# A state-space part stepped four tokens at a time, with prepared power matrices and a local term

## The reference, cut to what matters

```
lam_bar = jnp.exp(lam * dt)
b_bar = ((lam_bar - 1.0) / lam)[:, :, None] * b_mat
bu = jnp.einsum('gph,blgh->blgp', b_bar, u)
# states[t] = lam_bar * states[t-1] + bu[t]
y = jnp.einsum('ghp,blgp->blgh', c_mat, states).real
y = y + d_skip * u
y = jax.nn.gelu(y)
y = y * jax.nn.sigmoid(y @ w_glu + b_glu)
```

## Time and profile before

| | |
|---|---|
| median of three runs | 2754.56 us |
| lowest, highest | 2746.49, 2756.39 us |
| span of the profiled execution | 2747.2 us |
| its own time | only the span is given, inside the range of the runs |
| TensorE (PE) busy | 2600.3 us, 95% |
| VectorE (DVE) busy | 2165.5 us, 79% |
| ScalarE (ACT) busy | 1483.6 us, 54% |
| GpSimd (POOL) busy | 947.8 us, 34% |
| bytes moved by DMA | 670.58 MB, 243 GB/s from HBM over the span |

### The profile page before, as it was taken

One profiled execution on the slowest core, in us unless ns is written; L12 is line 12 of the kernel. 1 busy time (PEld: TensorE's weight loads), 2 busy tenths in 40 slices (PEclk: granted clock), 3 DMA queues, 4 the chain that ended last, 5 costly groups with the idle time before them and its releaser, 6 DMA issues. The chain is left out here.

```text
span 2747.2 us, 47482 instructions
## 1 busy us (share of the span) xinstructions
PE 2600.3 (95%) x17802; PEld 2379.0 (87%) x17802; DVE 2165.5 (79%) x2488; ACT 1483.6 (54%) x1930; POOL 947.8 (34%) x586
## 2 busy tenths in 40 slices
PE   8999899999998998888998978999999999999997
PEld 7999699999897998658998747999999999999986
DVE  5667666766787676987855997898989898989888
ACT  4337543443434334424334515777777777777765
POOL 6990089688789992126900130000000000000000
PEclk9999999999999998999999988999999999999999
DMA  8664267566566653324553415999999999999985
GB/s 309 252 237 148 103 241 256 202 250 254 191 241 229 220 183 134 115 105 164 183 184 138 164 63 192 343 350 333 352 335 349 338 347 343 347 345 346 340 320 216
DMA packets 129209, 670.58 MB, mean 244 GB/s; under 512 B 14672, under 2 KB 14992, under 8 KB 80064
## 3 DMA queue, kind: packets, MB, share of 16 engines
q1 hardware_dynamic: 111024, 604.72, 59.9%
q0 software_dynamic: 18064, 64.21, 6.9%
HBM read 667.82 MB, written 1.05 MB: 243 GB/s over the span
## 5 line engine op out<-in xcount | busy, mean ns | idle before, releaser
L1721 PE MATMUL work<-xT_hi,wh_gu 128*128 128x256 f32 x2088 | 593.9, 284 | 21.6 <-DVE xT_lo L985 12.0
L1722 PE MATMUL work<-xT_lo,wh_gu 128*128 128x256 f32 x2088 | 592.3, 284 | 0.0
L1723 PE MATMUL work<-xT_hi,wl_gu 128*128 128x256 f32 x2088 | 591.7, 283 | 0.0
L1721 PE MATMUL work<-wh_gu,mixT_hi 128*128 128x256 f32 x1792 | 507.5, 283 | 2.8 <-DVE wl_gu L1439 1.5
L1722 PE MATMUL work<-wl_gu,mixT_hi 128*128 128x256 f32 x1792 | 505.8, 282 | 0.0
L1723 PE MATMUL work<-wh_gu,mixT_lo 128*128 128x256 f32 x1792 | 505.5, 282 | 0.0
L857 DVE TENSOR_TENSOR wl_gu<-raw_gu,wh_gu 128x2048 fp32r<-128x2048 f32 x158 | 392.3, 2483 | 72.0 <-ACT wh_gu L395 71.5
L1721 PEld LDWEIGHTS work<-xT_hi,wh_gu 128*128 128x128 f32 x2088 | 401.3, 192 | 30.1 <-issue 21.3
L1722 PEld LDWEIGHTS work<-xT_lo,wh_gu 128*128 128x128 f32 x2088 | 401.7, 192 | 4.8
L1723 PEld LDWEIGHTS work<-xT_hi,wl_gu 128*128 128x128 f32 x2088 | 401.5, 192 | 0.0
L862 DVE TENSOR_TENSOR wl_d<-raw_d,wh_d 128x1024 fp32r<-128x1024 f32 x157 | 250.2, 1594 | 189.6 <-ACT wh_d L402 189.5
(11 more groups left out here) (436 smaller groups left out, 4785.6 us busy)
## 6 DMA issues: line engine op xcount, KB each, us to landing
raw_gu<-in_w_gu SPq DMA_DIRECT2D x271, 1024.0 KB, 5.2
raw_d<-in_w_d SPq DMA_DIRECT2D x269, 512.0 KB, 5.4
scratch<-in_w_gu SPq DMA_DIRECT2D x112, 1024.0 KB, 7.2
scratch<-in_w_d SPq DMA_DIRECT2D x112, 512.0 KB, 7.8
scratch<-in_w_mod POOLq DMA_DIRECT2D x96, 512.0 KB, 3.7
scratch<-in_s_b POOLq DMA_DIRECT2D x16, 256.0 KB, 2.9
rows<-in_norm_post POOLq DMA_DIRECT2D x6, 512.0 KB, 4.4
rows<-in_ln_g POOLq DMA_DIRECT2D x4, 512.0 KB, 5.5
```

Of the source, the lines that this page charges most:

```text
L1721: pe.matmul(out_, w[0], m[0], start=start, stop=False)
L1722: pe.matmul(out_, w[0], m[1], start=False, stop=False)
L1723: return pe.matmul(out_, w[1], m[0], start=False, stop=stop)
```

## The change

It takes the recurrence four tokens at a time (STEP = 4). With 64 blocks of four tokens c, the state behind each block is scanned with lam_bar^4, and

- the input of a block is one product of the four tokens' u (`U4`: 4 x 32 channels on 128 partitions, 64 columns) by B times lam_bar^(3-j) (`BF`),
- the output of a block is lam_bar^(i+1) times the factor and C (`CW`, 4 x 32 outputs) by the state behind the block before, plus a local term of the four tokens by each other, with D on its diagonal (`LOCAL`, 128 x 128 a tile), by `U4`.

`BF`, `LOCAL` and `CW` are prepared in the dense block before each mixer. For that the last 12 steps of the first of these dense blocks and the last 22 of the second are written out in place of the loop (`tail`); r counts back from the end of the first, and in the second everything comes ten steps earlier. Behind the gate/up product of step r, ahead of the down product:

- r = -11: TensorE transposes B (8 transposes), ScalarE keeps it (2 evictions of 512), and POOL multiplies it by lam_bar three times (18 operations of 512 elements).
- r = -7 to -4: TensorE waits for these powers, and transposes them, 8 a step (32), ScalarE keeps them, 2 evictions a step.
- r = -3: TensorE multiplies the powers by the scaled C: one 512-wide matmul for D, 32 of 32 columns. ScalarE keeps the result in steps -3 and -2, seven pieces each, and POOL makes `CW`, 24 operations of 512.

POOL loads B with eight and C with one DMA a layer and scales C (`s5_matrices`); the seven operations for it on VectorE go, and the DMAs for each round too. The table of angles has 64 columns in place of 256. It is built inside the mixer, after x is ready, beside the attention part (six doublings, seven squarings). Conversion of U+6 moves on VectorE from level 6 to behind the state-space part. The rest of the part is two halves h of eight state tiles:

- ScalarE `spread(h)`: 16 copies of 32 partitions by 2 x 64 out of PSUM into `U4`, after the table is there and after u0 and u1 (h = 0), u2 and u3 (h = 1). Blocks u2 and u3 lie in the banks of the output gate now, and wait for its Silu.
- TensorE `bu(h)`: 16 matmuls of 64 columns. VectorE `turn_in(h)`: four products of 8 x 64; `scan(h)`: two sums and 16 scans of 64; `turn_back(h)`: three operations; POOL the same three for the other component.
- TensorE `outputs(h)`: 8 matmuls of 64 and 16 of 63 columns.
- ScalarE `gathered_back(h)`: 16 Gelu pieces out of PSUM into `YT`, then the high part; VectorE its low part.

Buffers in scratch are laid out anew. The core of the diff:

```diff
+STEP = 4
+TAIL, LEAD = 12, 10
             def ffn(n0, dyn, nf, f0, fdyn):
+                tail = TAIL + LEAD * PREPARED.index(n0) if n0 in PREPARED else 0
...
+                for r in range(nf - tail, nf):
+                    gate_up(n0 + r)
+                    s5_products(PREPARED.index(n0), r - nf + LEAD * PREPARED.index(n0))
+                    down(n0 + r - 1, 0, f0 + r - 1, 0, False, False)
+                if tail:
+                    pe.wait_ge(s["local_sb"], 14 * (PREPARED.index(n0) + 1))
...
+            def s5_products(n, r):
+                if r == -11:
+                    pe.wait_ge(s5b_in, 128 * (n + 1))
+                    for c in range(2):
+                        for t in range(4):
+                            last = pe.transpose(PB[:, 2 + c, t * P:(t + 1) * P], BRAW[:, t, c, :], ident)
+                        last.then_inc(s["bt"], 1)
+                if -7 <= r <= -4:
+                    for k in (2 * r + 14, 2 * r + 15):
+                        c, st = turned_input(k)
+                        pe.wait_ge(s["powers"], n + 1)
+                        if k >= 2:
+                            pe.wait_ge(s["bf_sb"], 8 * n + k - 1)
+                        for i in range(4):
+                            last = pe.transpose(PB[:, 2 + k % 2, i * P:(i + 1) * P], stack(c, st.start + i), ident)
+                        last.then_inc(s["bf"], 1)
+                if r == -3:
+                    pe.wait_ge(s["bf_sb"], 8 * n + 7)
+                    pe.wait_ge(s["c_ready"], n + 1)
+                    pe.matmul(PB[:, 2, :], ONTO, SKIP, start=True, stop=False)
+                    for st in range(16):
+                        for c in range(2):
+                            last = pe.matmul(PB[:, 2, 32 * st:32 * st + 32], stack(c, st), CP[:, c, st, :],
+                                             start=False, stop=st == 15 and c == 1)
+                    last.then_inc(s["local"], 1)
...
+                def spread(h, used, count):
+                    act.wait_ge(s["table"], n + 1)
+                    act.wait_ge(used, count)
+                    ps = PA[:, 2 * h:2 * h + 2, 0:S].rearrange("p t (c j) -> p t j c", j=STEP)
+                    to = U4.rearrange("p (t q) c -> p t q c", q=4)
+                    for q in range(4):
+                        for j in range(STEP):
+                            act.activation(to[32 * j:32 * j + 32, 2 * h:2 * h + 2, q, :], ps[32 * q:32 * q + 32, :, j, :],
+                                           ACT.Copy).then_inc(s["u4"], 1)
...
+                dve.wait_ge(s["table"], n + 1)
                 turn_in(0)
-                for r in range(8):
...
+                scan(0)
+                dve.wait_ge(g["o"], n + 1)
+                turn_in(1)
+                gated_heads()
+                turn_back(0)
+                scan(1)
+                turn_back(1)
+                mixed_heads()
+                lo(U + 6)
+                lo(U + 7)
+                result_lo(0)
+                result_lo(1)
                 lo(U + 8)
...
                 bu(0)
                 heads()
                 bu(1)
                 heads_transposed()
                 r_ = [row_of(k) for k in (6, 7, 4, 5, 3, 0, 1, 2)]
-                for r in range(8):
...
+                outputs(0)
+                outputs(1)
+                pe.wait_ge(gu_lo, U + 7)
+                pe.wait_ge(s["bu_used"], 2 * (n + 1))
+                pe.wait_ge(mix_l, MSTART[b] + 2)
+                r_[0](U + 6, 0).then_inc(gu_used, 1)
                 pe.wait_ge(d_lo, U + 7)
                 r_[1](U + 6, 2).then_inc(d_used, 1)
-                pe.wait_ge(s["yl"], n + 1)
-                pe.wait_ge(s["ysum"], 4 * (n + 1))
+                pe.wait_ge(s["yl"], 2 * (n + 1))
```

More of the change, by code:

```diff
@@ L193, in program @@
         GO = first_net.rearrange("p (t d) -> p t d", t=NT)
[L194 to L204, removed]
+        OG = GO
+        PP = [[x.rearrange("p (t c) -> p t c", t=8) for x in half] for half in (
+            [view(1536 + 512 * i, 512) for i in range(5)] + [BT],
+            [ROW[:, 512 * i:512 * i + 512] for i in range(6)])]
+        YT = view(512, 1024).rearrange("p (k s) -> p k s", k=4)
         GL = view(2048, 1024).rearrange("p (k s) -> p k s", k=4)
@@ L517, in ffn, with step @@
             def ffn(n0, dyn, nf):
[L519 to L524, removed]
-                if n0 == 0:
-                    steps(0)
-                with act.Fori(1 if n0 == 0 else 0, nf // 2) as j:
-                    steps(dyn + j * 2)
+                def step(n, at):
+                    hi_gu(n + 1, at)
+                    ge(act, gu_used, n + 1, at)
+                    act.activation(SG[n % 2], PB[:, n % 2, 0:S], ACT.Silu).then_inc(silu_done, 1)
+                    hi_d(n + 1, at)
@@ L1079, in ffn @@
                     first, steps, reg = 1, chain.n, chain.reg
-                with dve.Fori(0, nf // 2 - first) as j:
+                tail = TAIL + LEAD * PREPARED.index(n0) if n0 in PREPARED else 0
+                looped = (nf - tail) // 2 - first
+                with dve.Fori(0, looped) as j:
                     chain.n, chain.reg = steps, reg + j * 4
@@ L1083, in ffn @@
                         step(r, j * 2)
-                chain.n, chain.reg = steps + 4 * (nf // 2 - first), reg
+                chain.n, chain.reg = steps + 4 * looped, reg
+                for r in range(nf - tail, nf):
+                    step(r, 0)
             mixed = [0]
@@ new lines, in scan @@
+                def scan(h):
+                    x = PP[h]
+                    dve.wait_ge(s["bu_used"], 2 * n + h + 1)
+                    TT(x[0], x[0], x[1], ALU.add)
+                    link(TT(x[2], x[2], x[3], ALU.subtract))
+                    for w in (x[0], x[2]):
+                        for t in range(8):
+                            at = 16 * n + 8 * h + t
+                            last = dve.tensor_tensor_scan(w[:, t, :], s5p[:, 1, at:at + 1].broadcast_to([P, S // STEP]),
+                                                          w[:, t, :], 0.0, ALU.mult, ALU.add)
+                    last.then_inc(s["states"], 1)
```

401 lines of the change are left out of this document (224 added, 177 removed).

## The result

The changed kernel takes 2755.89 us, the median of 18 runs; the kernel before takes 2748.09 us on the same chip, also of 18. The ratio is 1.0022, with an interval of [1.0015, 1.0029]: a little slower, and inside the 0.5% that the prediction called "the same". The forecast was 2724.6 us, so it missed by 31 us. The profiled execution has a span of 2751.7 us, 4.5 more than before.

A forecast was written before the change was run, and what follows sets the result against it. VectorE was taken to bound the two state-space parts, TensorE the rest. Per layer 15.7 us added and 30.9 removed, twice, gave -30 us: span 2747.2 to 2717, carried to the median 2754.56 as 2724.6; range 2704 to 2750.

The forecast's parts named there:

- The mechanism: State-space part: fewer, smaller VectorE operations let the gate matmuls start at 1611.2 in place of 1642.1, 30.9 us less a layer.
- third rival: Dense block: powers are late, 18 POOL operations at 3.1 us, TensorE waits 27 us, total 2775; chance 0.08.
- first rival: Attention part: POOL's table comes late beside VectorE, spreading late by 14 and 6 us, total 2745; chance 0.12.
- With 32 or 64 columns I take 0.11 a record: TensorE's narrow matmuls: 0.22 us a matmul, since the load of 128 weight columns binds already at one column.
- 5.3: State-space part: time in us for TensorE's 24 output matmuls of half 1.
- 1.6 is added: State-space part: us added to the outputs of half 1 for slow records behind TensorE's wait of some 4 us.
- 7.0: Dense block: us for the local term, one 512-wide matmul at 0.9 and 32 matmuls at 0.22.
- I take 0.2: ScalarE: us for each 128-element spreading copy, also used for the 16 Gelu pieces.
- second rival: Small pieces keep a fixed cost: scans 0.40, ScalarE pieces 0.36, adding 2 x 3.4 and 2.6 us a layer, 2743; chance 0.10.
- 2 us because the table of powers is now built on POOL beside the attention part: Attention part: 2 us added because POOL's table takes VectorE's turns; bounds 0 to 5.
- the Silu: Attention part: block u2 waits for the output gate's Silu, so 2.8 us are lost at once.
- The wait for the powers: Dense block: TensorE waits 2 us for POOL's 18 operations, 31 us in all; bounds 0 and 27.

The follow-up runs named there:

- e11: e10 with three 512-wide matmuls (result unused) behind the early local matmuls, ahead of the transposed heads: 2719.54 us, ratio 0.9865.
- e1: The changed kernel with ten unused 512-wide matmuls in TensorE's two gaps of each state-space part: 2750.74 us, ratio 1.0003.
- e3: The changed kernel with 28 of the 32 local-term matmuls left out in both preparing dense blocks: 2737.74 us, ratio 0.9953.
- e4: e1 with each half's 16 Gelu pieces replaced by one Gelu of 128 x 512, result columns in another order: 2744.95 us, ratio 0.9974.
- e9: The changed kernel with both mixers' tables built in the dense blocks ahead and the Silu between the last two exponentials: 2741.89 us, ratio 0.9958.
- e10: e9 with e6, e7, a row block between the output lists and a quarter of the gate matmuls ahead of the wait: 2717.75 us, ratio 0.9864.
- e6: The changed kernel with B transposed one step earlier and the local term in groups of 8, 12 and 12, evictions later: 2746.89 us, ratio 0.9972.
- e7: The changed kernel with the outputs' 16 local matmuls moved behind the inputs of half 1, into TensorE's gap: 2752.19 us, ratio 0.9992.

## Why the prediction was wrong

- **The mechanism was right.** 46.3 us against a forecast of 40.2, from 75.8; 16 scans in 3.02 us (3.1 said), half 1's outputs possible 27 us behind the last level (27.5 said), POOL's powers 32.1 us (31), eight transposes at full clock 1.04 us (0.96; the row of e11), the table in time. TensorE waited 3.2 us for the powers, not 27, so the third rival did not happen, nor did the first.
- **"With 32 or 64 columns I take 0.11 a record"** is the step that failed. It was read from a stretch at full clock and used wherever the matmuls stood. The outputs cost 0.425 a matmul: half 1 took 10.4 us where "5.3" and "1.6 is added" make 6.9. e1 gives back 5.7 us a layer. In the dense block the local term took 9.7 us ("7.0"), with 2.4 behind it that no term had; leaving out 28 of its 32 matmuls (e3) gives 9.7 a block. The prediction looked at the clock behind old waits, but those were followed by 256-wide matmuls, and it carried over how fast these recovered.
- **"I take 0.2" for ScalarE's pieces.** The spreading took 0.29, hidden as said. The Gelu took 0.41, above the rival's 0.36: from the end of the outputs to the gate matmuls 8.1 us, against 5.8 with the row blocks in the sum. The second rival's price was nearly right for ScalarE and wrong for the scans. In the changed kernel the slow row blocks hide all of it but 1.06 us; with the clock full it comes out (2.7 us, e4). Late start (0.3), outputs (3.5) and this tail (2.3) are the 6.1 us that the state-space part missed.
- **"2 us because the table of powers is now built on POOL beside the attention part".** Waits of 3.0 and 4.2 us came, with slow matmuls behind. Together with the Silu, whose 2.8 was exact, the parts lost 8.0 and 10.0, not 4.8; e9 takes 7 and 9 of it back. The contention the first rival spoke of was real, but it hit VectorE's products, not the date of the table.
- **The wait for the powers**: 3.2 us ("2"), again with a slow tail.
- Line by line the excess is 33 us over two layers, and 2 us of "rest", which varied by more than that between variants. About 10 us a layer of it are the clock, as an estimate from the figures above (outputs 3.5, local term and the down product behind it 5.1, tail behind the powers 1.7); so with the clock priced right the sum would still have been more than 10 us too low, by the attention parts, the Gelu pieces and the wait.
- The base was off as well. The prediction carried over a median of three runs, 7.4 us above the span; here the median is 4.2 above it. So the miss of 31 us in the median is one of 35 in the span.
- The range ended at 2750: it held rivals for each price alone, and none in which one cause, the clock, raised several terms at once.

## What to carry to other kernels

Before full-width matmuls are swapped for many narrow ones, price them at both clock levels and ask what TensorE does just ahead of them: here an idle of 5.46 us in front made 48 of them cost double, until something wide ran. Put narrow groups between wide products, and put real work with no dependence into the gap; in e10 that work was a row block, and it ran its first 2.7 us at half speed itself. An operation that is moved in one engine's list delays what stands behind it there, and so another engine: the evictions of e6 and e10 made new waits of 3.9 and 2.4 us. Work moved to an idle engine is free only where its neighbour on the same memory is idle too; here the idle place was the dense block, not the attention part.

## What the runs showed of the hardware

- Matmuls with 64 moving columns kept a full clock without a gap (13.6 us in e7: inputs, local matmuls, the heads' 128 columns between them), yet a low clock did not rise while they ran (20.7 us at 0.50). In the local term, 32 columns and no gap, the clock fell within 9.65 us; in groups of 16 to 24 records between wide products it stayed at 1.00 (e6).
- The narrow record is 0.11 us at full clock and 0.21 at the low one, so what bounds it slows with the clock.
- A 128 x 256 product of VectorE is 0.41 us alone and up to 1.50 beside POOL's 512-element products, which then range from 1.05 to 3.10.
- A piece of 32 partitions by 128 elements out of PSUM costs ScalarE 0.29 (copy) or 0.41 (Gelu), and VectorE 0.41. A scan of 64 costs VectorE 0.19, one of 256 0.61.
